# Modulation blocks requested evenly beside the first feed-forward output's units, and added on VectorE ahead of the tiles' squares

## The reference, cut to what matters

```
# end of the first block
y = (gelu(gate) * val) @ w_ffn_out          # 2816 -> 1024
h = h + rmsnorm(y, norm_ffn_post)
# start of the second block
c_act = silu(c)
mod = c_act @ w_ada + b_ada                 # 1024 -> 6 * 1024
sh_m, sc_m, g_m, sh_f, sc_f, g_f = split(mod, 6)
h = modulate(rmsnorm(x, norm_mix_g), sh_m, sc_m)
```

## Time and profile before

| what | value |
|---|---|
| time, median of 3 runs | 1690.85 us (1687.84 to 1692.06) |
| time of the profiled execution | 1686.82 us |
| its span in the trace | 1685.0 us |
| TensorE busy | 1579.1 us of the span |
| first `ffn_out`: first matmul to first small matmul behind it | 699.05 to 841.29 us |
| second `ffn_out`, the same 528 matmuls | 122.82 us from 1547.15 us |

### The profile page before, as it was taken

How to read it: one execution, slowest core, us unless ns; L and a number is a source line. 1 busy time by engine, 2 the same in 40 slices (tenths; PEclk the granted TensorE clock), 3 DMA queues, 4 the chain that set the end, 5 groups by cost and what they waited for, 6 DMA issues and landing times.

```text
span 1685.0 us, 20836 instructions
## 1 busy us (share of the span) xinstructions
PE 1579.1 (94%) x8734; PEld 1337.0 (79%) x8734; DVE 848.6 (50%) x1081; ACT 629.9 (37%) x1008; POOL 564.1 (33%) x231
## 2 busy tenths in 40 slices
PE   4979989989799999998899998999988999999996
PEld 4978878879699999976668865777876888888885
DVE  3233033341788888854459947874355334432122
ACT  4451053373443333322342235344544323333221
POOL 2321011104144444443504432321442434444441
PEclk9989589969899999999979999999998999999998
DMA  4211012102122222566512321211221333332332
GB/s 174 88 51 39 13 38 85 40 12 89 42 96 88 88 98 91 187 227 233 202 43 94 100 73 42 74 51 38 95 81 63 125 112 105 109 125 88 105 107 75
DMA packets 43628, 155.32 MB, mean 92 GB/s; under 512 B 4848, under 2 KB 5488, under 8 KB 43536
## 3 DMA queue, kind: packets, MB, share of 16 engines
q1 hardware_dynamic: 42960, 151.51, 26.6%
q10 hardware_dynamic: 576, 2.49, 0.4%
HBM read 151.89 MB, written 2.10 MB: 91 GB/s over the span
## 4 chain that ended last, share of the span: by engine, by line
PE 82%; DVE 7%; ACT 6%; DMA 3%; issue 2%; SPq 0%; POOL 0%; DVEq 0%; ACTq 0%
PE G L410 69%; DMA raw<-wstream 2%; DVE ada_acc L1714 2%; PE G L552 2%; PE B L859 1%; PE B L387 1%; PE B L879 1%; PE G L645 1%; PE B L771 1%; PE B L604 1%; PE G L546 1%; ACT whi L956 1%; PE G L647 1%; PE B L621 1%; PE B L530 1%
## 5 line engine op out<-in xcount | busy, mean ns | idle before, releaser
L367 POOL TENSOR_TENSOR wlo<-raw,whi 128x1024 fp32r<-128x1024 f32 x227 | 563.9, 2488 | 1092.9 <-ACT whi L956 1092.7
L410 PE MATMUL G<-uhi,whi 128*128 128x258 f32 (+4 forms) x1920 | 542.0, 335 | 37.1 <-DVE ulo L1439 12.3
L410 PE MATMUL G<-ulo,whi 128*128 128x258 f32 (+4 forms) x1920 | 530.2, 329 | 0.0
L410 PE MATMUL G<-uhi,wlo 128*128 128x258 f32 (+4 forms) x1920 | 528.8, 328 | 0.0
L410 PEld LDWEIGHTS G<-uhi,whi 128*128 128x128 f32 x1920 | 327.9, 194 | 104.0 <-issue 67.0
L410 PEld LDWEIGHTS G<-uhi,wlo 128*128 128x128 f32 x1920 | 328.6, 194 | 30.1
L410 PEld LDWEIGHTS G<-ulo,whi 128*128 128x128 f32 x1920 | 328.8, 194 | 27.9
L956 ACT ACTIVATE whi<-raw 128x1024 fp32r<-128x1024 f32 x227 | 239.4, 1055 | 224.1 <-DMA raw<-wstream 224.0
L410 PE MATMUL G<-yhi,whi 128*128 128x512 f32 x352 | 141.8, 403 | 12.8 <-POOL wlo L367 12.8
L410 PE MATMUL G<-yhi,wlo 128*128 128x512 f32 x352 | 140.8, 400 | 0.0
L410 PE MATMUL G<-ylo,whi 128*128 128x512 f32 x352 | 140.8, 400 | 0.0
(11 more groups left out here) (266 smaller groups left out, 1646.9 us busy)
## 6 DMA issues: line engine op xcount, KB each, us to landing
raw<-wstream SPq DMA_DIRECT2D x227, 512.0 KB, 3.3
ada_in<-ada SPq DMA_DIRECT2D x40, 512.0 KB, 5.5
ada_late<-ada SPq DMA_DIRECT2D x8, 512.0 KB, 3.8
h<-hT SPq DMA_DIRECT2D x8, 264.0 KB, 4.8
out<-res SPq DMA_DIRECT2D x8, 256.0 KB, 2.2
biasn<-bias SPq DMA_DIRECT2D x2, 960.0 KB, 11.0
biasn<-bias ACTq DMA_DIRECT2D x2, 960.0 KB, 5.6
scan_keep<-scanm SPq DMA_DIRECT2D x1, 528.0 KB, 8.7
```

What stands on the lines that cost most here:

```text
L367: pool.tensor_tensor(wlo[:, i, :], raw[:, i, :], whi[:, i, :].bitcast(F32), ALU.subtract)\
L410: ins = pe.matmul(dst[:, x, 0:xw], w[:, slot, b * P:(b + 1) * P], u[:, k, off + x0:off + x0 + xw], start=(first and i == 0 and j == 0), st ...
```

## The change

Three places change. SyncE used to issue two modulation blocks behind every unit of the stage; it now issues them at 5 blocks in 3 units, by a new function `ada_by(j)`, which says how many are requested once j units beyond the first have been. VectorE used to take 8 blocks before it added the squares of tiles 0 and 1, and 6 more before each next tile; it now takes as many as `ada_by(3k + 5)` says before tile k's squares: 18, 23, 28, 33, 38, 40, 40. ScalarE used to round unit 3c + 5 before it copied tile c; it now rounds only unit 3c + 4 before the copy, and unit 3c + 5 between the copy and the square.

```diff
+def ada_by(j):
+
+    return min(ADA_EARLY, ADA_RING + 5 * j // 3)
...
                 elif j >= 1:
-                    for x in range(ADA_RING + 2 * j - 2, min(ADA_EARLY, ADA_RING + 2 * j)):
+                    for x in range(ada_by(j - 1), ada_by(j)):
                         load_ada(x)
...
             for c in range(KD):
                 t = T0["ffn_out"] + c
-                hi_through(U0["ffn_out"] + 3 * c + RING + 1)
+                hi_through(U0["ffn_out"] + 3 * c + RING)
                 act.wait_ge(s["unit_used"], U0["ffn_out"] + 3 * c + 3)
                 act.activation(m2[:, c, :], G[:, t % 2, 0, :], ACT.Copy).then_inc(s["evac_done"], 1)
+                hi_through(U0["ffn_out"] + 3 * c + RING + 1)
                 act.wait_ge(s["evac_done"], t + 1)
                 square("ffn_post", c, m2[:, c, :])
...
             for k in range(1, KD):
-                while x < min(ADA_EARLY, KD + 6 * (k - 1)):
+                while x < ada_by(3 * k + 5):
                     part = x // KD
```

## The result

| | changed kernel | before |
|---|---|---|
| time, median | 1668.49 us (1663.38 to 1672.20, 4 runs) | 1689.78 us (1687.84 to 1692.06, 4 runs) |
| ratio | 0.9871, 95% interval 0.9838 to 0.9905 | |
| profiled execution, its span | 1672.20 us, 1670.4 us | 1686.82 us, 1685.0 us |

The account below looks back on a forecast made before the run. TensorE was taken as the bound, busy 94% of the span, losing 19.4 us in the first `ffn_out`. -19.4 + 0.8 = -18.6 us gave 1668.2 or 1672.2 by base; forecast 1671.5 us, range 1666 to 1681.

Parts of the forecast that it names:

- the ring: First `ffn_out`: VectorE, SyncE's queue, transfers and ScalarE wait in a circle, 20.05 us a round against TensorE's 15.35 a tile.
- The measure of the loss: First `ffn_out` takes 142.24 us, the second, with the same 528 matmuls, 122.82; so 19.4 us can be gained.
- VectorE fits, near the upper bound of collisions: In the stage, VectorE's work per tile is 8.5 to 15.0 us, near the upper end, below TensorE's 15.35.
- one chance in ten: VectorE steps wait out whole GpSimd splits, 15.7 us a tile; VectorE becomes the bound, costing 3 us in all.
- ScalarE has 2.6 us to spare: Path through the held square to unit 3c + 6's split takes 16.9 us of 19.5, so TensorE never waits.
- The last tile, 0.8 us: Behind the stage, rounding unit 26 before the last square makes TensorE's sum of the norm wait 0.8 us longer.
- Between 1668.2 and 1672.2: Whole kernel: 18.6 us off the profiled execution gives 1668.2, off the median 1672.2; forecast 1671.5 us, nearer the median.
- Rival A: In the stage, the held square still delays units at tiles 4 to 7; time 1676 to 1686 us, chance 0.18.
- Rivals B and C: B: VectorE becomes the bound, 1707 us, chance 0.04; C: transfers replace the wait, 1686 to 1692 us, chance 0.06.

Follow-up runs that it names:

- one more unit's blocks: Changed kernel, but VectorE takes the blocks of one more unit before each addition of squares; stage 122.93 us, time 1671.53 us (1 run).
- two more units' blocks: Changed kernel, but VectorE takes the blocks of two more units before each addition of squares; stage 128.83 us, time 1669.89 us (1 run).

## Why the prediction was right, step by step

The mechanism was right: the ring opened and TensorE got all of the 19.4 us back. One term of the sum was not: the tail behind the stage cost 3.4 us and not 0.8. So S became 16.0 us shorter, where the sum has 18.6.

- **The measure of the loss** (19.4 us from the second `ffn_out`): 19.4 us measured, in every kernel whose ring was open and that had no further change to the stage.
- **The ring** of VectorE's order, SyncE's queue and ScalarE's square: shown. Taking out either of the first two is enough, which the prediction did not say. It did not ask whether ScalarE's part is needed: that part adds nothing to the gain, and it costs 1.7 us behind the stage.
- **VectorE fits, near the upper bound of collisions**: right in kind. The mean of a step rose from 1.63 to 2.32 us, with 20 of 35 steps stretched. VectorE was busy for 99.1 us of 122.87 and waited for blocks for 18.7 us. But the reason given, that the two engines share the loss, was a misreading. In each collision one engine takes all of it: the one that starts second waits until the other has ended. The step at 741.85 us waited out nearly a whole split; it lasted 3.37 us and not 1.27 + 2.40 = 3.67, since it began 0.11 us behind the split and ended only 1.08 behind it. The addition did the same: its 0.69 us became 2.44, behind a last split that ran from 823.06 to 825.42 us. The trace of before had it too: its additions of 1.80 to 1.86 us each ended 0.55 us behind the split that they met. So what the prediction gave one chance in ten was so in kind, but it did not make VectorE the bound. That is what the Trainium skill states (page "SBUF — State Buffer", section "SBUF: two separate sides"), that the loser blocks for the winner's whole instruction. This case's trace agrees, and so does the run with the sum in PSUM, for a step, with its condition of two SBUF inputs.
- **ScalarE has 2.6 us to spare**: it has 4.8, and the run with one more unit's blocks shows that over 4 us are there. Blocks landed in 6.1 us in the median, over the 5.5 taken. But in the tile shown above only one step stood between the last landing and the addition, 2.65 us where the sum has 4.7 for two, and the addition took 0.68 and not 1.65:

```profile
747.21 2.65 DVE L1720 SCALAR_TENSOR_TENSOR ada_acc<-ada_in,small,ada_acc 128x1024 f32<-128x1024 f32 x1 [1.33 <-DMA ada_in<-ada]
```

- **The last tile, 0.8 us**: this is the term that was mis-sized; it measured 3.4 us. Its parts: the norm's sum started 4.60 us behind the last matmul and not 4.25, because the addition met nearly a whole split (1.14 us late against before). The rest goes with TensorE's clock, for which the prediction had no term: the norm's sum took 2.07 us in place of 0.97, the three groups 10.03 in place of 9.48, and mix2's sums 10.37 where the chain of before has 9.74. 1.14 + 1.10 + 0.55 + 0.63 = 3.42 us. In the stretch 824.19 to 826.00 us of the kernel without ScalarE's order the norm's sum ran at a granted clock of 0.51, and took 1.83 us where before it took 0.97 at 1.00. Comparing S, 1.7 of the 3.4 us go with ScalarE's order, and 1.7 are there without it. Why the clock falls some microseconds earlier behind the shorter stage, though TensorE's work ahead of it is the same, is open. The norm's sum of before, by stretch:

```profile
844.75:845.72 0.97, 0.97 (x6) 0.49 (x5) 0.00 (x0) 0.00 (x0) 0.00 (x0) 1.00 0.05 21
```

- **Between 1668.2 and 1672.2**: the medians came at 1668.5 and 1670.2. That the first came under the forecast of 1671.5, although the tail cost 2.6 us more than forecast, counts as luck: the 16.0 us of S, taken from the medians of before (1689.78 and 1688.81), would give 1673.8 and 1672.8. What is missing, 5.3 and 2.6 us, lies outside the stretch, where executions of one kernel scatter by as much (below), and no run names a cause of it in the change.
- **Rival A**: its path is real, as the run with two more units' blocks shows, but the changed kernel keeps 4.8 us off it.
- **Rivals B and C**: no run shows either. VectorE had idle time, and the queues carried 274 GB/s with blocks landing in 6.1 us.

## What to carry to other kernels

When a stage loses time and no engine in it is full, follow the chain of waits until it closes. If it is a ring, look for the member that can be taken out most cheaply, try the members alone, and leave the others as they are. Hold a background load (here the modulation blocks) by what its own loads allow, not by a result of the stage it runs beside; and if it shares a queue with the stage's loads, ask for it only when its buffer is surely free. A twin of the stage without the disturbance, elsewhere in the same trace, is a good measure of what can be won: here the twin's 122.82 us were reached within 0.05.

## What the runs showed of the hardware that I had not expected

TensorE's clock fell while its records show it busy. In the kernel without ScalarE's order it went through 32 rows of small matmuls, one column each, with their weight loads, and was at the lower of its levels right behind them (columns as in the earlier trace rows):

```profile
822.40:824.19 1.79, 1.79 (x18) 1.79 (x18) 1.61 (x1) 0.00 (x0) 1.07 (x1) 1.00 0.58 220
824.19:826.00 1.81, 1.81 (x5) 0.78 (x4) 0.00 (x0) 0.00 (x0) 0.00 (x0) 0.51 0.02 7
```

The moment is not fixed. Before, the same 32 rows and the norm's sum behind them ran at 1.00. In the changed kernel the clock fell amid those rows:

```profile
823.00:824.50 1.50, 1.50 (x11) 1.50 (x11) 0.96 (x1) 0.50 (x1) 1.44 (x1) 0.69 0.70 259
```

Part of the scatter of one kernel's time arises far from the change. In two profiled executions of the changed kernel the stage began at 698.55 and at 693.12 us. At the start of ScalarE's fourth table load they stand at 127.87 and 128.51 us, at that of the fifth at 216.34 and 210.89. From 150 to 200 us TensorE is busy throughout in both, and the clock differs, 0.59 in the first and 0.70 in the second:

```profile
150.00:200.00 50.00, 50.00 (x254) 44.50 (x255) 7.42 (x21) 3.53 (x8) 3.72 (x2) 0.59 0.03 12
```

```profile
150.00:200.00 50.00, 50.00 (x288) 44.32 (x286) 8.07 (x21) 3.53 (x8) 4.35 (x2) 0.70 0.05 16
```

Not all of the scatter is there: the two profiled executions without ScalarE's order begin the stage within 0.2 us of each other and differ by 3.4 us behind S.

Two inputs in SBUF are not the only condition for the stretch. A `TENSOR_SCALAR`, with its one block in SBUF and its sum written there, is stretched too: 0.74 us at its shortest and 2.71 at its longest in the changed kernel, where before none of five was over 0.75. Written to PSUM it took 1.29 us and was never stretched.
